# Two edits of a two-block transformer kernel: where the stage areas start, and how the gated linear attention's output products are ordered

## The chip, the cores and the metric

One core of one Trainium2 chip runs the whole program. The metric is the device time of one execution in microseconds (us), lower is better.

## The reference

Two blocks run one after the other on x [1, 512, 1024], all in fp32. The first has two hybrid layers, the second a pooling layer and an attention layer. Cut to what matters here:

```python
def hybrid_layer(x, ...):                       # twice
    h = modulate(rms_norm(x, norm1_g), shift1, scale1)
    rq..rg, gq, gk, gv, glr, gg, fq, fk, fv, ff = split(h @ w_in)
    ret   = silu(rg) * head_group_norm(retention(rq, rk, rv))
    gla_o = silu(gg) * rms_norm(gla(gq, gk, gv, log_a))     # 4 heads, key width 64, value width 128
    fox_o = forgetting_attention(...)
    mixed = sum(sigmoid(h @ w_mg + b_mg) * (branches @ w_br)) @ w_o
    x = x + gate1 * mixed
    u, g = split(h2 @ w_up)
    x = x + gate2 * ((silu(causal_dwconv(u)) * g) @ w_down)

def gla(q, k, v, log_a):                        # chunks of 64 positions
    ...
    _, s_all = lax.scan(step, zeros, (a, kv))   # state after each chunk, 64 x 128 a head
    o = einsum('bnihd,bnhde->bnihe', qc, s_all) # 8 chunks x 4 heads
```

The second block has the same shape of work: norm, mixer, residual, norm, SwiGLU of width 2816, residual.

## The kernel before

Activations lie transposed: 128 features down the partitions and all 512 positions along the row, eight such tiles for 1024 features. The program is written five times over, once for each engine (`TensorSteps`, `ScalarSteps`, `VectorSteps`, and `pool_program`, `sync_program`). One `schedule` walks the first three through the same list of generator steps, so the order of every queue is fixed by the order of the calls.

**Dense products.** Each fp32 product is split in three: a weight tile has a high part `hi` and a low part `lo`, an activation tile as well (`HH`, `HL` for the normed input; others below), and `dot` (L410 to L412) issues hi·high, hi·low and lo·high, each with a 128x128 stationary tile and a moving tile of 512 or 256 columns of type fp32r. SyncE loads weights into a ring of six slots (`raw`), ScalarE copies them to `hi` (L1152), GpSimd subtracts to `lo` (L2463).

**Where tiles lie.** `places` puts the long-lived tiles one after another with `fixed`, each rounded up to 32 bytes, and then a region of 49 x 2048 bytes from `big` on, in which `area(name, tile, ...)` gives every stage its own tiles at `big + tile * 2048`. In the built program `HH` begins at byte 32,896 of each partition, `HL` at 49,280 and `hi` at 90,240, all multiples of 128. `big` is 128,864, which is 1006 x 128 + 96. In the areas are, among others, the moving operands `FH`/`FL` (input of w_down), `ErH`/`ErL`, `EgH`/`EgL`, `EfH`/`EfL` (the three branches), `MH`/`ML` (input of w_o), `PH`/`PL`, `ZH`/`ZL` (pooling) and `YH`/`YL` (attention output).

**Gated linear attention, last part** (`gla_attention`). `weave` gives one step of the gate projections (`gated(l, 0)`, 8 steps) after each step of this generator; the 8 are used up by the time the output products begin, so these have no dense work between them. The four heads lie in pairs: head h uses pair `p2 = h // 2` and row half `hh = h % 2` (partitions 0 to 63 or 64 to 127) of the states `SA` and queries `gq`. A head's output takes 8 matmuls (one for each chunk, 64 rows, 128 stationary columns, 64 moving columns, plain fp32) into PSUM bank `s0` or `s1` (L812). The profile records each plain fp32 matmul twice. Then ScalarE squares the bank into one of two buffers of `glaS` (L1452) and VectorE copies it to `GO` (L2091), TensorE sums the squares by 4 matmuls against `ones` (`colsq`, L486), ScalarE takes the root into `RS` (L1192), VectorE inverts it (L2095), and TensorE spreads it over the partitions (`spread`, L495). The square of head h waits for the sum of head h - 2, whose buffer it takes, and head h's products wait until `GO` of head h - 2 is copied, whose bank they take. When the stage is over, `gated(l, 1)` goes on with dense products.

Of the kernel before, what the change touches and what calls it, by code (L numbers as in the profile page):

```python
# [9 lines left out]
ACT = mybir.ActivationFunctionType  # L10
# [220 lines left out]
class Steps:  # L231
# [8 lines left out]
    def next_chunk(self, pair=False):  # L240
        n = self.n
        if pair and n % NSLOT == NSLOT - 1:
            n += 1
        self.n = n + 1
        return n


def ret_jobs(l):
# [131 lines left out]
class TensorSteps(Steps):  # L380
# [390 lines left out]
    def gla_attention(self, l):  # L771
        e, q, m, t, bank, free = self.e, self.q, self.m, self.t, self.bank, self.free
        LA = t["LA"]
        yield from self.gla_gates(l)
        for u in range(2):
            q.wait_ge(m.vattn.at("la", l, u), free[f"t{u}"])
            for r in range(2):
                mm = e.matmul(bank[f"t{u}"][:, r * 256:r * 256 + 256], t["tail"][:, :], LA[:, u, r * 256:r * 256 + 256],
                              start=True, stop=True)
            mm.then_inc(*m.attn.up(("gd", l, u)))  # L780
            free[f"t{u}"] = m.aattn.at("gd", l, u)
        q.wait_ge(free["s0"])
        for f2 in range(2):
            for r in range(4):
                mm = e.matmul(bank["s0"][:, f2 * 8 + 2 * r:f2 * 8 + 2 * r + 2],
                              LA[:, r // 2, (r % 2) * 256 + f2 * 128:(r % 2) * 256 + f2 * 128 + 128],
                              t["chunk"][:, :], start=True, stop=True)
        mm.then_inc(*m.attn.up(("ga", l)))
        free["s0"] = m.aattn.at("ga", l)
        yield None  # L790
        yield None
        kvb = ("s0", "s1", "t0", "t1")
        for p2 in range(2):
            q.wait_ge(m.vattn.at("gk", l, 0), m.vattn.at("gk", l, 1),
                      *[m.atake.at("gv", l, c, u) for c in range(2) for u in range(2)], *[free[b] for b in kvb])
            for n in range(8):
                c0, r = 64 * (n % 2), n // 2
                mm = e.matmul(bank[kvb[n % 2 + n // 4 * 2]][:, (n // 2 % 2) * 256:(n // 2 % 2) * 256 + 256],
                              t["ED"][c0:c0 + 64, r // 2, (r % 2) * 256 + p2 * 128:(r % 2) * 256 + p2 * 128 + 128],
                              t["gv"][c0:c0 + 64, r, p2 * 256:p2 * 256 + 256], start=True, stop=True)  # L800
            mm.then_inc(*m.attn.up(("gkv", l, p2)))
            for b in kvb:
                free[b] = m.vattn.at("gs", l, p2, 7, 1)
            yield None
        yield None
        for h in range(4):
            p2, hh = h // 2, h % 2
            b = f"s{hh}"
            r = slice(64 * hh, 64 * hh + 64)
            q.wait_ge(m.vattn.at("gs", l, p2, 7, 1), m.atake.at("gq", l, p2), free[b])  # L810
            for n in range(8):
                mm = e.matmul(bank[b][:, n * 64:n * 64 + 64], t["SA"][r, p2, n, :], t["gq"][r, p2, n * 64:n * 64 + 64],  # L812
                              start=True, stop=True)
            mm.then_inc(*m.attn.up(("go", l, h)))
            free[b] = m.vattn.at("go", l, h)
            yield None
            if h >= 1:
                self.gla_sum(l, h - 1)
        self.gla_sum(l, 3)
        free["t1"] = m.aattn.at("gsd", l)  # L820
        yield None
        for h in range(4):
            b = f"t{h % 2}"
            self.spread(t["RS"][:, 4 * h:4 * h + 4], b, m.vattn.at("gr", l), ("gspread", l, h))
            free[b] = m.vattn.at("GO", l, h)
            yield None
# [308 lines left out]
class ScalarSteps(Steps):  # L1135
# [289 lines left out]
    def gla_attention(self, l):  # L1425
        e, q, m, t, bank = self.e, self.q, self.m, self.t, self.bank
        TA, ED, AD, SQ = t["TA"], t["ED"], t["AD"], t["glaS"]
        yield None
        for u in range(2):
            q.wait_ge(m.attn.at("gz", l, u))  # L1430
            e.activation(TA[:, u, :], bank[f"s{u}"][:, :], ACT.Abs).then_inc(*m.aattn.up(("gabs", l, u)))
        for u in range(2):
            q.wait_ge(m.aattn.at("gabs", l, u))
            e.activation(TA[:, u, :], TA[:, u, :], ACT.Exp, scale=-1.0).then_inc(*m.aattn.up(("gexp", l, u)))
        for u in range(2):
            q.wait_ge(m.aattn.at("gexp", l, u))
            e.activation(TA[:, u, :], TA[:, u, :], ACT.Ln, bias=t["one"][:, 0:1]).then_inc(*m.aattn.up(("gln", l, u)))
        yield None
        yield None
        for u in range(2):  # L1440
            q.wait_ge(m.attn.at("gd", l, u))
            e.activation(ED[:, u, :], bank[f"t{u}"][:, :], ACT.Exp, scale=1.0 / 16).then_inc(*m.aattn.up(("gd", l, u)))
        q.wait_ge(m.attn.at("ga", l))
        e.activation(AD[:, 0:16], bank["s0"][:, 0:16], ACT.Exp, scale=1.0 / 16).then_inc(*m.aattn.up(("ga", l)))
        yield None
        yield None
        yield None
        yield None
        yield None
        for h in range(4):  # L1450
            q.wait_ge(m.attn.at("go", l, h), m.stat.at("gsum", l, h - 2) if h >= 2 else None)
            e.activation(SQ[:, h % 2, :], bank[f"s{h % 2}"][:, :], ACT.Square).then_inc(*m.aattn.up(("gsq", l, h)))  # L1452
            yield None
        self.rstd(bank["t1"], 16, 128, m.stat.at("gsum", l, 3), t["RS"][:, 0:16], m.aattn.up(("gsd", l)))
        yield None
        for h in range(4):
            yield None
# [267 lines left out]
class VectorSteps(Steps):  # L1725
# [329 lines left out]
    def gla_attention(self, l):  # L2055
        e, q, m, t, bank = self.e, self.q, self.m, self.t, self.bank
        LA, TA, ED, AD, SA, GO = t["LA"], t["TA"], t["ED"], t["AD"], t["SA"], t["GO"]
# [14 lines left out]
        for p2 in range(2):  # L2072
            q.wait_ge(m.attn.at("gkv", l, p2), m.aattn.at("ga", l))
            for n in range(8):
                for hh in range(2):
                    r = slice(64 * hh, 64 * hh + 64)
# [11 lines left out]
        yield None  # L2088
        for h in range(4):
            q.wait_ge(m.aattn.at("gsq", l, h))  # L2090
            e.tensor_copy(GO[:, h, :], bank[f"s{h % 2}"][:, :]).then_inc(*m.vattn.up(("go", l, h)))  # L2091
            yield None
        RS = t["RS"][:, 0:16]
        q.wait_ge(m.aattn.at("gsd", l))
# [428 lines left out]
def places(nc):  # L2523
    with ExitStack() as ctx:
# [3 lines left out]
        at = [base]  # L2528
        t = {}

        def fixed(name, shape, dt=F32):
            n = int(np.prod(shape[1:])) * 4
            t[name] = nc.alloc_sbuf_tensor_at(name, shape, dt, offset=at[0])
            at[0] += (n + 31) // 32 * 32
# [23 lines left out]
        fixed("NA", [128, 4, 8])  # L2558
        fixed("aG", [128, 24])
        fixed("AA", [128, S])  # L2560
        big = at[0]
        assert big + 49 * TB <= nc.sbuf_usable_end, big + 49 * TB - nc.sbuf_usable_end

        def area(name, tile, shape, dt=F32):
# [74 lines left out]
        bank = {b: ctx.enter_context(nc.psum_tensor(b, [128, S], F32))  # L2639
                for b in ("b0", "b1", "b2", "s0", "s1", "t0", "t1", "o")}  # L2640
        return ctx.pop_all(), t, raw, bank

def build(nc, I, T, out):
    stack, t, raw, bank = places(nc)
    with stack as ctx:
        marks = Marks(lambda name: ctx.enter_context(nc.semaphore(name)))
        K = Kernel(I, T, out, marks, raw, t, bank)
        for program in (tensor_program, scalar_program, vector_program, pool_program, sync_program):
            program(Rehearsal(), K)
        for mark in marks.all():  # L2650
            mark.begin()
        block = ctx.enter_context(nc.Block())

        @block.sync
        def _(e):
            sync_program(e, K)

        @block.tensor
        def _(e):
            tensor_program(e, K)  # L2660

        @block.vector
        def _(e):
            vector_program(e, K)

        @block.scalar
        def _(e):
            scalar_program(e, K)

        @block.gpsimd  # L2670
        def _(e):
            pool_program(e, K)
# [37 lines left out]
```

## Time and profile before

| what | value |
|---|---|
| device time, 3 runs | 3119.80, 3119.99, 3122.06 us (median 3119.99) |
| the profiled execution | 3121.84 us, its span 3120.1 us |
| mean granted TensorE clock | 0.983 |
| TensorE matmul busy / weight load busy | 97% / 81% |
| VectorE, ScalarE, GpSimd busy | 34%, 35%, 38% |
| HBM traffic | 100 GB/s over the span |

The profiled time is 1.7 us longer than the span, which lies around the first and the last instruction. Matmuls overlap, so the duration of one says little; what counts is the distance from one start to the next. L numbers are lines of the kernel before; in the changed one the same code stands 3 to 7 lines further down.

### The profile page before, as it was taken

Reading aid. Unit: us, or ns where it says so; the run is one execution under the profiler, and the core shown is the slowest. Engines: PE = TensorE matmul, PEld = TensorE weight load, DVE = VectorE, ACT = ScalarE, POOL = GpSimd, SP = SyncE. Lnnn points to the kernel's source line nnn. Section 1 sums busy time; section 2 is a strip of 40 time slices with the busy share of each in tenths; the row PEclk is TensorE's granted clock in tenths of the full one; section 3 lists DMA queues with packets and bytes.
Section 4 is the critical chain, followed back from the end, with each engine's and each line's share of the span. In section 5 each row is a group of like instructions: output and inputs, shape, how many; then the busy total and the mean of one; then the engine's idle time right before and its main releaser. Section 6 shows DMA issues by size and latency. Waiting matters only on the chain.

```text
span 3120.1 us, 36402 instructions
## 1 busy us (share of the span) xinstructions
PE 3026.0 (97%) x15435; PEld 2523.2 (81%) x15435; DVE 1056.4 (34%) x1867; ACT 1079.0 (35%) x1643; POOL 1181.2 (38%) x502
## 2 busy tenths in 40 slices
PE   7999999999999999999999999979999999999999
PEld 4887788898888888778888888868888877788887
DVE  2633451255554532231143220463110255531102
ACT  3424333243332433432234332323222266432321
POOL 1422144434445432224434444434444333344442
PEclk9999899999999999989999999989999999999999
DMA  6331253335555422223333333323333322233332
GB/s 208 108 92 51 82 170 100 88 106 184 189 186 169 111 69 61 55 61 95 95 88 101 95 96 95 93 68 95 95 97 91 97 69 67 61 95 95 100 89 75
DMA packets 523798, 315.30 MB, mean 101 GB/s; under 512 B 15954, under 2 KB 496884, under 8 KB 523380
## 3 DMA queue, kind: packets, MB, share of 16 engines
q1 hardware_dynamic: 523636, 312.98, 34.0%
q8 instruction: 122, 2.00, 0.3%
q14 instruction: 40, 0.33, 0.0%
HBM read 310.84 MB, written 2.10 MB: 100 GB/s over the span
## 4 chain that ended last, share of the span: by engine, by line
PE 92%; DVE 4%; ACT 2%; DMA 1%; issue 0%; SPq 0%; ACTq 0%; DVEq 0%
PE b L410 21%; PE b L412 20%; PE b L411 20%; PE o L410 5%; PE o L411 5%; PE o L412 5%; DMA raw<-in_w_in_dram 1%; PE b L451 1%; PE b L452 1%; PE b L453 1%; PE b L555 1%; PE o L727 1%; ACT aT L1283 1%; PE t L495 1%; PE s L812 1%; PE s L621 1%
## 5 line engine op out<-in xcount | busy, mean ns | idle before, releaser
L2463 POOL TENSOR_TENSOR lo<-raw,hi 128x1024 fp32r<-128x1024 f32 (+1 forms) x492 | 1179.1, 2404 | 1900.4 <-ACT hi L1152 1900.1
L410 PE MATMUL b<-HH,hi 128*128 128x512 f32 x1776 | 707.5, 398 | 15.1 <-ACT aT L1283 10.5
L412 PE MATMUL b<-HH,lo 128*128 128x512 f32 x1776 | 694.7, 391 | 0.0
L411 PE MATMUL b<-HL,hi 128*128 128x512 f32 x1776 | 694.3, 391 | 0.0
L1152 ACT ACTIVATE hi<-raw 128x1024 fp32r<-128x1024 f32 (+1 forms) x492 | 508.8, 1039 | 453.9 <-DMA raw<-in_w_down_dram 107.9
L410 PEld LDWEIGHTS b<-HH,hi 128*128 128x128 f32 x1776 | 335.1, 189 | 92.1 <-issue 19.6
L412 PEld LDWEIGHTS b<-HH,lo 128*128 128x128 f32 x1776 | 334.8, 189 | 71.1
L411 PEld LDWEIGHTS b<-HL,hi 128*128 128x128 f32 x1776 | 335.4, 189 | 69.1 <-issue 1.0
L410 PE MATMUL b<-FH,hi 128*128 128x512 f32 (+1 forms) x572 | 212.1, 371 | 0.0
L411 PE MATMUL b<-FL,hi 128*128 128x512 f32 (+1 forms) x572 | 211.4, 370 | 0.0
L412 PE MATMUL b<-FH,lo 128*128 128x512 f32 (+1 forms) x572 | 211.3, 369 | 0.0
L2191 DVE TENSOR_TENSOR CB<-CB,b 128x512 f32<-128x512 f32 x82 | 56.4, 688 | 455.1 <-PE b L412 441.7
L410 PE MATMUL o<-HH,hi 128*128 128x512 f32 x496 | 193.4, 390 | 0.0
L411 PE MATMUL o<-HL,hi 128*128 128x512 f32 x496 | 193.2, 390 | 0.0
L412 PE MATMUL o<-HH,lo 128*128 128x512 f32 x496 | 193.2, 390 | 0.0
L1538 ACT ACTIVATE FH<-CB 128x512 fp32r<-128x512 f32 x88 | 55.6, 632 | 253.7 <-DVE CB L2191 253.7
L410 PE MATMUL b<-hi,HH 128*128 128x256 f32 x480 | 142.8, 297 | 0.4 <-ACT aT L1283 0.4
L411 PE MATMUL b<-lo,HH 128*128 128x256 f32 x480 | 137.4, 286 | 0.0
L412 PE MATMUL b<-hi,HL 128*128 128x256 f32 x480 | 137.2, 286 | 0.0
L1869 DVE SCALAR_TENSOR_TENSOR AA<-raw,CA,AA 128x512 f32<-128x512 f32 x140 | 127.8, 913 | 4.1
L410 PEld LDWEIGHTS b<-FH,hi 128*128 128x128 f32 x572 | 107.7, 188 | 20.0
L412 PEld LDWEIGHTS b<-FH,lo 128*128 128x128 f32 x572 | 107.7, 188 | 19.9
(414 smaller groups left out, 4649.8 us busy)
## 6 DMA issues: line engine op xcount, KB each, us to landing
raw<-in_w_ada_dram SPq DMA_DIRECT2D x96, 512.0 KB, 4.9
raw<-in_w_up_dram SPq DMA_DIRECT2D x88, 512.0 KB, 3.9
raw<-in_w_in_dram SPq DMA_DIRECT2D x80, 512.0 KB, 4.2
raw<-in_w_mg_dram SPq DMA_DIRECT2D x48, 512.0 KB, 3.7
raw<-in_ffn_w_gate_dram SPq DMA_DIRECT2D x44, 512.0 KB, 3.8
raw<-in_ffn_w_up_dram SPq DMA_DIRECT2D x44, 512.0 KB, 3.8
raw<-in_w_down_dram SPq DMA_DIRECT2D x32, 512.0 KB, 3.9
raw<-in_ffn_w_down_dram SPq DMA_DIRECT2D x32, 512.0 KB, 3.9
```

The lines of the kernel that those rows point to most:

```text
L410: e.matmul(out, wh, xh, start=start and k == 0, stop=False)
L411: e.matmul(out, wh, xl, start=False, stop=False)
L412: mm = e.matmul(out, wl, xh, start=False, stop=stop and k == last)
L451: e.matmul(out[:, c], hi[:, k, :], t["HH"][:, k, c], start=(k == 0), stop=False)
L452: e.matmul(out[:, c], hi[:, k, :], t["HL"][:, k, c], start=False, stop=False)
L453: mm = e.matmul(out[:, c], lo[:, k, :], t["HH"][:, k, c], start=False, stop=(k == 7))
L495: mm = e.transpose(self.bank[b][:, r * 128:r * 128 + 128], bc(cols[:, r:r + 1], 128), self.t["ident"][:, :])
L1152: e.activation(t["hi"][:, c % NSLOT, 0:w], K.raw[:, c % NSLOT, 0:w], ACT.Copy).then_inc(*m.hi.up(c))
L1538: e.activation(t["FH"][:, f, :], CB[:, b, :], ACT.Copy).then_inc(*m.atake.up(("fh", i, f)))
L1869: a = e.scalar_tensor_tensor(out=AA[:, :], in0=raw[:, k * 512:k * 512 + 512], scalar=CA[:, kk:kk + 1], in1=AA[:, :], op0=ALU.mult, op1=ALU ...
L2191: e.tensor_tensor(CB[:, b, :], CB[:, b, :], self.out_of(key)[:, :], ALU.mult).then_inc(*m.vtake.up(key))
L2463: e.tensor_tensor(t["lo"][:, s, 0:w], K.raw[:, s, 0:w], t["hi"][:, s, 0:w].bitcast(F32), ALU.subtract).then_inc(*m.lo.up(n))
```

## The change

Two edits. The first rounds `big` up to the next multiple of 128, so every area tile begins 32 bytes later (`FH` at 128,896 = 1007 x 128). The second lets the output products of a head pair alternate: chunk n of the lower row half, then chunk n of the upper. The first pair writes `s0` and `s1`, the second `t0` and `o`, so it no longer waits for the copies of the first pair. All sums of squares come after all products. ScalarE and VectorE keep their order and only read other banks.

```diff
+GLA_BANKS = ("s0", "s1", "t0", "o")
...
-        for h in range(4):
-            p2, hh = h // 2, h % 2
-            b = f"s{hh}"
-            r = slice(64 * hh, 64 * hh + 64)
-            q.wait_ge(m.vattn.at("gs", l, p2, 7, 1), m.atake.at("gq", l, p2), free[b])
+        for p2 in range(2):
+            both = GLA_BANKS[2 * p2:2 * p2 + 2]
+            q.wait_ge(m.vattn.at("gs", l, p2, 7, 1), m.atake.at("gq", l, p2), free[both[0]], free[both[1]])
             for n in range(8):
-                mm = e.matmul(bank[b][:, n * 64:n * 64 + 64], t["SA"][r, p2, n, :], t["gq"][r, p2, n * 64:n * 64 + 64],
-                              start=True, stop=True)
-            mm.then_inc(*m.attn.up(("go", l, h)))
-            free[b] = m.vattn.at("go", l, h)
-            yield None
-            if h >= 1:
-                self.gla_sum(l, h - 1)
+                for hh, b in enumerate(both):
+                    r = slice(64 * hh, 64 * hh + 64)
+                    mm = e.matmul(bank[b][:, n * 64:n * 64 + 64], t["SA"][r, p2, n, :],
+                                  t["gq"][r, p2, n * 64:n * 64 + 64], start=True, stop=True)
+            mm.then_inc(*m.attn.up(("go", l, 2 * p2), ("go", l, 2 * p2 + 1)))
+            for hh, b in enumerate(both):
+                free[b] = m.vattn.at("go", l, 2 * p2 + hh)
+            yield None
+        self.gla_sum(l, 0)
+        self.gla_sum(l, 1)
+        yield None
+        self.gla_sum(l, 2)
+        yield None
         self.gla_sum(l, 3)
...
-            e.activation(SQ[:, h % 2, :], bank[f"s{h % 2}"][:, :], ACT.Square).then_inc(*m.aattn.up(("gsq", l, h)))
+            e.activation(SQ[:, h % 2, :], bank[GLA_BANKS[h]][:, :], ACT.Square).then_inc(*m.aattn.up(("gsq", l, h)))
...
-            e.tensor_copy(GO[:, h, :], bank[f"s{h % 2}"][:, :]).then_inc(*m.vattn.up(("go", l, h)))
+            e.tensor_copy(GO[:, h, :], bank[GLA_BANKS[h]][:, :]).then_inc(*m.vattn.up(("go", l, h)))
...
-        big = at[0]
+        big = (at[0] + 127) // 128 * 128
```

TensorE's queue in the kernel before, at the output products of the first layer (the digit in a bank's name tells it from the others, the digits behind `gq`, `SA`, `ones` and `glaS` only number the tiles):

```order
1474 L812 MATMUL s0<-gq_111,SA_112 128x64 x8
1475 L812 MATMUL s1<-gq_111,SA_112 128x64 x8
1476 L486 MATMUL t1<-ones_58,glaS_121 128x1 x4
1477 L812 MATMUL s0<-gq_111,SA_112 128x64 x8
1478 L486 MATMUL t1<-ones_58,glaS_121 128x1 x4
1479 L812 MATMUL s1<-gq_111,SA_112 128x64 x8
1480 L486 MATMUL t1<-ones_58,glaS_121 128x1 x8
```

The same place in the changed kernel:

```order
1474 L815 MATMUL s0<-gq_111,SA_112 128x64
1475 L815 MATMUL s1<-gq_111,SA_112 128x64
...
1489 L815 MATMUL s1<-gq_111,SA_112 128x64
1490 L815 MATMUL t0<-gq_111,SA_112 128x64
1491 L815 MATMUL o<-gq_111,SA_112 128x64
...
1505 L815 MATMUL o<-gq_111,SA_112 128x64
1506 L489 MATMUL t1<-ones_58,glaS_121 128x1 x16
1507 L498 MATMUL t0<-CON_56,RS_61 128x128 x4
```

The 32 products are the same ones, in another order and with two other banks, and the 16 sums that stood between and behind them now all stand behind them.

## Rows read from the trace of the kernel before

**Rows 1.** The page's section 4: the chain that ended last, by engine.

```profile
PE 92%; DVE 4%; ACT 2%; DMA 1%; issue 0%; SPq 0%; ACTq 0%; DVEq 0%
```

**Rows 2.** Timeline of PE, area tiles, 512 columns: start us, us, instruction; 59 rows between.

```profile
2999.83 0.40 PE L410 MATMUL b<-FH,hi 128*128 128x512 f32 x1
...
3013.83 0.39 PE L410 MATMUL b<-FH,hi 128*128 128x512 f32 x1
```

**Rows 3.** Timeline of PE, HH and HL, 512 columns; 59 rows between.

```profile
2899.84 0.39 PE L412 MATMUL o<-HH,lo 128*128 128x512 f32 x1
...
2913.44 0.39 PE L412 MATMUL b<-HH,lo 128*128 128x512 f32 x1
```

**Rows 4.** Timeline of PE, area tiles, 256 columns; 49 rows between.

```profile
640.92 0.28 PE L410 MATMUL b<-MH,hi 128*128 128x256 f32 x1
...
646.83 0.28 PE L412 MATMUL b<-MH,lo 128*128 128x256 f32 x1
```

**Rows 5.** Timeline of PE, HH and HL, 256 columns; 49 rows between.

```profile
1640.15 0.28 PE L451 MATMUL b<-HH,hi 128*128 128x256 f32 x1
...
1646.15 0.28 PE L453 MATMUL b<-HH,lo 128*128 128x256 f32 x1
```

**Rows 6.** Groups of PE by line and form: xcount | busy us, mean ns | idle before us <-releasers.

```profile
L410 PE MATMUL b<-FH,hi 128*128 128x512 f32 x440 | 174.5, 396 | 0.0
...
L410 PE MATMUL o<-FH,hi 128*128 128x512 f32 x176 | 69.8, 397 | 0.0
```

**Rows 7.** Groups of DVE by line and form, an area tile and `X`, which begins at a multiple of 128.

```profile
L2135 DVE TENSOR_TENSOR SG<-b,SG 128x512 f32<-128x512 f32 x32 | 22.1, 691 | 186.1 <-PE b L412 186.1
...
L1771 DVE TENSOR_TENSOR X<-b,X 128x512 f32<-128x512 f32 x18 | 12.5, 692 | 167.5 <-PE b L412 152.0 <-PE b L907 15.4
```

**Rows 8.** The chain in order of time, a full-height fp32 product of 256 columns.

```profile
337.84 1.73 PE t L778 x8
```

**Rows 9.** Timeline of PE, layer 1: half-height products whose row halves alternate.

```profile
1322.70 1.13 PE L798 MATMUL s<-gv,ED 64*128 64x256 f32 x8
1323.67 1.03 PE L798 MATMUL t<-gv,ED 64*128 64x256 f32 x8
1324.63 0.50 PE L410 MATMUL b<-HH,hi 128*128 128x512 f32 x1
```

**Rows 10.** Timeline of PE, layer 1's output products and sums.

```profile
1339.93 3.39 PE L812 MATMUL s<-gq,SA 64*128 64x64 f32 x32
1343.25 1.05 PE L486 MATMUL t<-ones,glaS 128*128 128x1 f32 x8
1344.23 2.96 PE L812 MATMUL s<-gq,SA 64*128 64x64 f32 x16
...
1352.52 3.57 PE L486 MATMUL t<-ones,glaS 128*128 128x1 f32 x16
```

**Rows 11.** Timeline of ACT, layer 1, squares and root; [idle before <-releaser].

```profile
1345.69 0.58 ACT L1452 ACTIVATE glaS<-s 128x512 f32<-128x512 f32 x1
...
1356.13 0.27 ACT L1192 ACTIVATE RS<-t,eps 128x16 f32<-128x16 f32 x1 [1.60 <-PE t L486]
```

**Rows 12.** Timeline of PE, layer 0, and the spreads that follow.

```profile
364.24 3.39 PE L812 MATMUL s<-gq,SA 64*128 64x64 f32 x32 [0.15 <-DVE SA L2083]
...
383.71 3.93 PE L495 MATMUL t<-CON,RS 128*128 128x128 f32 x16 [0.65 <-DVE RS L2095]
```

**Rows 13.** Timeline of ACT, layer 0.

```profile
371.60 0.58 ACT L1452 ACTIVATE glaS<-s 128x512 f32<-128x512 f32 x1
...
383.09 0.27 ACT L1192 ACTIVATE RS<-t,eps 128x16 f32<-128x16 f32 x1 [1.60 <-PE t L486]
```

**Rows 14.** Stretches: us, PE PEld DVE ACT POOL busy (x), PEclk, DMA share, GB/s.

```profile
1344.50:1345.50 1.00, 1.00 (x9) 1.00 (x9) 0.62 (x1) 0.35 (x1) 0.07 (x1) 0.77 0.00 0
...
1345.50:1360.00 14.50, 13.85 (x62) 12.99 (x63) 4.57 (x8) 5.75 (x8) 2.35 (x1) 0.50 0.00 1
368.00:370.00 2.00, 0.61 (x6) 0.52 (x5) 1.97 (x2) 0.00 (x0) 1.16 (x1) 0.71 0.00 0
```

## The prediction

> **What bounds the kernel now.** I read the chain of work that ended last first: 92% of it is TensorE and waiting for nothing, so the span is the sum of what TensorE issues plus a few stalls [rows 1]. What counts is therefore the distance between starts of the most frequent instructions, and what TensorE waits for where it has no dense work. Both edits concern one of these.
>
> For the distances I took stretches of the timeline in which TensorE runs without a gap. With a moving operand from an area (`FH`, `FL`), 60 steps take 3013.83 - 2999.83 = 14.00 us, or 233.3 ns for each product of 512 columns [rows 2]. With `HH` or `HL` as the moving operand, in the same code with the same kind of weights, 60 steps take 2913.44 - 2899.84 = 13.60 us, or 226.7 ns [rows 3]. With 256 columns it is the other way round: area tiles take 5.91 us for 50 steps, 118.2 ns [rows 4], and `HH` and `HL` 6.00 us, 120.0 ns [rows 5]. Among the wide ones, what sets the two apart in the kernel's own terms is where the tile lies: `HH` and `HL` begin at a multiple of 128 bytes, all area tiles 96 bytes past one. They also lie lower in memory; the trace can't separate the two.
>
> For the stall I read the output products of the gated linear attention. In layer 1 TensorE issues 32 records for heads 0 and 1, 8 for the first sum, 16 for head 2, and so on; the last two sums end 3.57 us after 1352.52 [rows 10], and the root on ScalarE starts at 1356.13 [rows 11]. No dense product stands in between. The granted clock was 0.77 in the stretch 1344.50 to 1345.50, and 0.50 from there to 1360.00: it fell from the 2.4 GHz level to 1.2 GHz at about 1345.0, after some 5 us of these small products [rows 14]. Layer 0 is alike, with the fall between 368 and 370, at about 368.8 by its mean of 0.71 [rows 14].
>
> **The start of the areas.** Nothing is added or removed; each area tile moves by 32 bytes. Wide products with an area operand: `FH` alone stands in 440 + 176 groups of three [rows 6], 1,848 products; counted in the program, the three branches add 576, `MH`/`ML` 240, `ZH`/`ZL` 120, `YH`/`YL` 120, `PH`/`PL` 48: 2,952. If each takes the distance of `HH`, it saves 233.3 - 226.7 = 6.6 ns, together 19.5 us. The bounds are nothing (if the cause lies elsewhere) and 6.6 ns; I take 6.6, since code, weights, type and width are the same and only the tile differs. Narrow products with an area operand number 1,104 (the same tiles in the last output tiles, done in halves). By the nearest rows they go from 118.2 to 120.0 ns, a loss of 1.8 ns each or 2.0 us; the other bound is no change. I take the loss. All these products lie on the chain. For VectorE the start seems not to matter: 691 ns for a sum in an area, 692 for one in `X`, which is at a multiple of 128 [rows 7]; and both are hidden behind TensorE in most of the span. Net for this edit: 19.5 - 2.0 = 17.5 us.
>
> A rule speaks against it. The Trainium skill, "SBUF — State Buffer", section "Door 1: The DMA port swizzle", says that SBUF is read in lines of 16 bytes and that a penalty falls due on crossing to a new line. Byte 128,864 is as good a multiple of 16 as 128,896, so by that rule a contiguous row costs the same before and after, and this edit would bring 0. The sum by the rows goes by the 6.6 ns that they show.
>
> **The alternating products.** The plain fp32 products of full height and 256 columns take 1.73 us for 8 records, 0.216 us each [rows 8]. Those of half height whose halves alternate take 1324.63 - 1322.70 = 1.93 us for 16 records, 0.121 each [rows 9], 1.8 times as fast. So two halves do run beside each other. The output products now take 1343.25 - 1339.93 = 3.32 us for 32 records, 0.104 each [rows 10], with one half after the other. Bounds for the alternating ones are 0.104 (no overlap) and 0.104 x 0.121 / 0.216 = 0.058. I take 0.058, because rows 9 have the same height and the same stationary width: 32 records in 1.9 us.
>
> The Trainium skill, "TensorEngine Tiling (Array Packing)", section "Key Properties", says that tiles of the array are independent, each loading weights and multiplying in parallel. Rows 9 agree, at 1.8 times rather than 2.
>
> Layer 1, step by step. Products of all four heads from 1339.93 take 2 x 1.9 = 3.8 us, to 1343.7; the banks of the second pair are free, so nothing is waited for. The sum of head 0 takes 1344.23 - 1343.25 = 0.98 us [rows 10], to 1344.7. The sum of head 1 waits for its square, which starts at 1345.69 and takes 0.58, to 1346.27 [rows 11]. That square waits in ScalarE's queue for work on the gate tile, not for TensorE, and neither ScalarE's nor VectorE's order changes, so it stays where it is. Then three sums at half clock, 3.57 / 2 = 1.79 us for 8 records [rows 10], end at 1346.27 + 5.37 = 1351.64. The squares of heads 2 and 3 lie beside them: head 3's may start when head 1's sum is done and is needed 1.79 us later. The root then starts at 1351.7 instead of 1356.13: 4.4 us saved. What is late next is again the chain of sums, each behind the other on TensorE.
>
> Layer 0. The products start at 364.24 [rows 12] and would be done with the first sum near 369; the square of head 1 ends at 371.60 + 0.58 = 372.18, three sums end at 377.55, the root starts at 377.6 instead of 383.09 [rows 13]: 5.5 us saved. The spreads and all behind them move up unchanged. Cover: the second pair's products cost nothing as long as they end before head 1's square does, with 1.6 us to spare in layer 1 and 3 in layer 0. Without that cover (no overlap of halves), in layer 1 5.1 of 6.64 us run before the clock falls and the other 1.5 take 3.1, so the products end near 1348.1 and four sums of 1.79 at 1355.3, which saves 0.8; in layer 0, by the same steps, 3.0.
>
> Sum: 17.5 + 4.4 + 5.5 = 27.4 us. The profiled execution took 3121.84, so it becomes 3094.4. Its time is 1.85 above the median of the three runs; against that, 3119.99 - 27.4 = 3092.6, which I round to 3093.
>
> **Rivals.**
> (A) The start doesn't matter, and `HH` is faster for another reason, such as its place in memory. For it: the trace has no tile that differs in its start alone, and the narrow products rank the other way. Against: all area tiles have one distance whatever their offset in the region. Only the products' order counts: 3119.99 - 9.9 = 3110.1. The rule on 16-byte lines leads here too.
> (B) The halves don't overlap at 64 columns, because loading 128 stationary columns is what takes the 0.104 us and only streams overlap. Rows 9 don't refute that fully, as a stream of 256 columns is longer. Saved: 17.5 + 0.8 + 3.0 = 21.3, time 3098.7.
> (C) Slower: a start at a multiple of 128 costs wide products something, as the narrow ones' rows suggest (+1.8 ns), instead of helping. It decides the sign from (9.9 - 2.0) / 2,952 = 2.7 ns for each wide product; at 6.6 the wrong way the time is 3119.99 - 9.9 + 2.0 + 19.5 = 3131.6.
> (D) The clock doesn't fall in the shortened stage. Three sums then take 2.9 us instead of 5.4 and the spreads, 3.93 us at half clock [rows 12], 2.0 less: 4.4 more a layer, 8.8 together, time 3083.8. Against: TensorE waits for head 1's square longer than before, and does no dense work there.
>
> **How the numbers follow.** The forecast has 0.72, with its own range of 3089 to 3098 (1 ns more or less for each wide product, no loss on the narrow ones, a microsecond of the stage). A has 0.12, B 0.07, D 0.06, C 0.02, A and B together 0.01 (3119.99 - 3.8 = 3116.2). A range of 3083 to 3104 takes in the forecast, B and D and a saving on wide products of two thirds, and leaves out 0.15. A measurement of this kernel tells about 0.2%, 6.2 us, from no change. Faster by more: forecast, A, B, D, 0.97. Within: A with B, 0.01. Slower: C, 0.02.
>
> **What the profile would show.** First edit right: 60 steps with `FH` in 13.6 us, and 50 narrow steps in 6.0. If 14.0 stands, A holds. Second: the 32 product records of a pair in about 1.9 us and 64 in one piece; a wait of 1.6 us in layer 1 and 3 in layer 0 for the square of head 1; then 24 sum records in 5.4 us at a granted clock of 0.50; the root 11.8 us behind the first product in layer 1 and 13.4 in layer 0. Products in 3.3 us a pair would be B. Wrong altogether if the square of head 1 moved with the products, or if weights came late to the faster products; SyncE's loads now wait for slots to come free, so I expect none.

## The result, and the profile after

The changed kernel takes 3093.58 us (median of 4 runs, 3091.97 to 3096.79); the kernel before took 3119.89 in the same session. The ratio is 0.991, with a 95% interval of 0.9898 to 0.9923. The forecast was 3093, in a range of 3083 to 3104. The profiled execution took 3096.79 us, its span 3095.0, against 3121.84 and 3120.1.

TensorE still carries the chain, as in [rows 1]:

```profile
PE 92%; DVE 4%; ACT 2%; DMA 1%; issue 1%; SPq 0%; ACTq 0%; DVEq 0%
```

The timeline of PE, area tiles with 512 columns, 60 steps from the first row to the last:

```profile
2358.38 0.39 PE L413 MATMUL b<-FH,hi 128*128 128x512 f32 x1
...
2371.98 0.39 PE L413 MATMUL o<-FH,hi 128*128 128x512 f32 x1
```

That is 13.60 us, 226.7 ns a step, where [rows 2] had 14.00 us; area tiles now go at the pace that `HH` had in [rows 3]. The same view with 256 columns, 50 steps:

```profile
1594.13 0.28 PE L415 MATMUL o<-MH,lo 128*128 128x256 f32 x1
...
1600.13 0.28 PE L414 MATMUL b<-ML,hi 128*128 128x256 f32 x1
```

6.00 us, 120.0 ns, where [rows 4] had 5.91: the small loss came as well. Groups of PE by line and form show the first in sum (busy us, mean ns):

```profile
L413 PE MATMUL b<-FH,hi 128*128 128x512 f32 x440 | 171.5, 390 | 0.0
...
L413 PE MATMUL o<-FH,hi 128*128 128x512 f32 x176 | 68.7, 390 | 0.0
```

They were 174.5 and 69.8 [rows 6]. Overlapping durations add up to more than the time they cover, but here they fell as the distances did: 3.0 us over 440 is 6.8 ns each.

The stage of the output products, timeline of PE, layer 0 and then layer 1 (only the first row of a pair of banks that alternates is shown; the second pair follows in single rows, to 368.08 in layer 0):

```profile
364.56 2.00 PE L815 MATMUL s<-gq,SA 64*128 64x64 f32 x32
...
368.28 1.05 PE L489 MATMUL t<-ones,glaS 128*128 128x1 f32 x8
371.84 5.28 PE L489 MATMUL t<-ones,glaS 128*128 128x1 f32 x24 [2.51 <-ACT glaS L1459]
377.78 3.92 PE L498 MATMUL t<-CON,RS 128*128 128x128 f32 x16 [0.65 <-DVE RS L2102]
...
1329.12 2.00 PE L815 MATMUL s<-gq,SA 64*128 64x64 f32 x32 [0.34 <-DVE SA L2090]
...
1332.83 1.05 PE L489 MATMUL t<-ones,glaS 128*128 128x1 f32 x8
1335.58 4.54 PE L489 MATMUL t<-ones,glaS 128*128 128x1 f32 x24 [1.69 <-ACT glaS L1459]
```

All 64 records of the products take 3.72 us in layer 0 (364.56 to 368.28); before, 32 of them took 3.32 [rows 10]. Then TensorE sums head 0 and waits, 2.51 and 1.69 us, for the square of head 1. ScalarE's timeline of layer 0 shows what that square stands behind:

```profile
366.61 0.60 ACT L1459 ACTIVATE glaS<-s 128x512 f32<-128x512 f32 x1 [0.48 <-PE s L815]
367.10 0.59 ACT L1474 ACTIVATE GT<-b 128x512 f32<-128x512 f32 x1
370.68 0.63 ACT L1476 ACTIVATE ErH<-GT 128x512 fp32r<-128x512 f32 x1 [2.98 <-DVE GT L2119]
371.21 0.58 ACT L1459 ACTIVATE glaS<-s 128x512 f32<-128x512 f32 x1
...
377.17 0.28 ACT L1199 ACTIVATE RS<-t,eps 128x16 f32<-128x16 f32 x1 [1.52 <-PE t L489]
```

Both squares had their input at 366.6; the second waits for two operations on the gate tile, and the latter of these for VectorE, 2.98 us. The root comes 12.61 us behind the first product (377.17 - 364.56). Before, it came 18.85 behind [rows 12, 13]: 6.24 saved. In layer 1 it comes 11.04 behind (1340.15) instead of 16.20 [rows 10, 11]: 5.17 saved. The first dense product moves up by the same amounts, 23.05 to 16.80 and 20.39 to 15.23 us behind the first output product.

Stretches around the fall of the clock (PEclk is the third number from the end):

```profile
368.00:370.00 2.00, 1.33 (x16) 1.18 (x12) 1.97 (x3) 0.00 (x0) 0.77 (x1) 1.00 0.00 1
370.00:381.00 11.00, 8.50 (x38) 7.89 (x39) 5.09 (x10) 5.99 (x8) 2.35 (x1) 0.52 0.17 48
...
1335.00:1337.00 2.00, 1.43 (x11) 1.43 (x11) 1.89 (x3) 1.28 (x4) 0.00 (x0) 0.86 0.00 0
1337.00:1341.00 4.00, 3.35 (x16) 3.26 (x17) 0.95 (x2) 2.46 (x4) 0.00 (x0) 0.50 0.00 0
```

The granted clock still fell from the 2.4 GHz level to 1.2 GHz. By the means it fell at about 370.4 (a mean of 0.52 over 11 us is 0.44 us at full clock and the rest at half) and 1336.4 (0.86 over 2 us: 1.44 at full), 5.9 and 7.3 us behind the first product, where it had been 4.6 and 5.1 [rows 14]. In both layers TensorE was waiting, or had just waited, for the square of head 1.

Over the whole trace, adding up distances from start to start, in us: wide area products 695.0 to 676.6, -18.4, and another -0.7 in two waits of over 3 us among them; narrow area products +1.6; narrow ones with `HH` and `HL` -1.4; those whose moving operand is a weight tile -0.9; wide ones with `HH` and `HL` +3.5 (their usual distance is 227 ns in both; 139 steps against 123 lie between 300 and 500 ns, as at half clock); the two stages -11.4. That is -27.7. The spans differ by 25.1, so everything else took 2.6 us more.

### The profile page after: what moved, and what is told of

Its sections match the earlier page's. It is cut to its first block, busy times and chain, and to the rows that moved or that the text cites. A ratio compares the mean times of both kernels' runs of the same rounds, so it can differ in the third digit from the quotient of the medians.

```text
span 3095.0 us, 36400 instructions
## 1 busy us (share of the span) xinstructions
PE 2999.5 (97%) x15435; PEld 2510.9 (81%) x15435; DVE 1053.0 (34%) x1867; ACT 1079.1 (35%) x1643; POOL 1179.3 (38%) x502
## 4 chain that ended last, share of the span: by engine, by line
PE 92%; DVE 4%; ACT 2%; DMA 1%; issue 1%; SPq 0%; ACTq 0%; DVEq 0%
PE b L413 21%; PE b L415 20%; PE b L414 20%; PE o L413 5%; PE o L415 5%; PE o L414 5%; DMA raw<-in_w_in_dram 1%; PE b L454 1%; PE b L455 1%; PE b L456 1%; PE b L558 1%; PE o L730 1%; DVE SA L2090 1%; ACT aT L1290 1%; PE t L498 1%; DVE W L2232 1%
## 5 line engine op out<-in xcount | busy, mean ns | idle before, releaser
L414 PEld LDWEIGHTS b<-FL,hi 128*128 128x128 f32 x572 | 107.9, 189 | 17.2
```

What stands on the lines that cost most here:

```text
L414: e.matmul(out, wh, xl, start=False, stop=False)
```

## The experiments

All diffs are against the changed kernel unless said otherwise. Times are medians, and each ratio is to the kernel before, run in the same session (3119.9 to 3123.0 us). "Distance" in time is from one product's start to the next, in a mean over a trace's wide products, without gaps of 300 ns or more; for narrow products the text gives the middle value of the trace. In time, two executions of one kernel differ by up to 12.8 us (the kernel before, 3115.04 to 3127.79), so small differences rest on the intervals, not on single runs.

### The two edits apart

**Areas only**, the kernel before with one line changed:

```diff
-        big = at[0]
+        big = (at[0] + 127) // 128 * 128
```

> The kernel before with the areas' start rounded up alone. If the two edits add and the start is worth 6.6 ns on 2,952 wide products less 1.8 ns on 1,104 narrow ones: 17.5 us less than before, about 3102; 60 steps of wide products with FH take 13.6 us and the root of the output stage stays 16.2 and 18.9 us behind the first product. If the start gives nothing by itself: 3120 and 14.0 us.

3103.75 us (4 runs), ratio 0.9942, interval 0.9925 to 0.9958. Wide area products 226.9 ns, narrow ones 120. 0.0058 of 3119.9 is 18 us; the forecast's term was 17.5. The stage is unchanged, yet the root comes 18.74 and 17.23 us behind the first product, where the kernel before had 18.85 and 16.20: in layer 1 the clock fell 3.9 us behind the first product here and 5.1 there. So one trace's stage can differ by a microsecond with nothing changed in it.

**Products only**, the changed kernel without that line:

```diff
-        big = (at[0] + 127) // 128 * 128
+        big = at[0]
```

> The changed kernel with the areas where they were before. If the stage alone gives what the two traces show between first product and root (16.2 to 11.0 us in layer 1, 18.9 to 12.6 in layer 0): 11.4 us less than before, about 3108.5, and 60 steps with FH stay at 14.0 us. If the stage's gain is given back later: 3115 or more.

3114.24 us (9 runs), ratio 0.9975, interval 0.9965 to 0.9985. Wide area products 233.3 ns, as before; root 12.86 and 11.36 us behind, dense products 17.05 and 15.55. The trace saves 6.0 and 4.8 us, the ratio says 8 (5 to 11). The two edits add within the intervals: 0.0058 + 0.0025 = 0.0083, against 0.0090 for both.

### What in the order of the products saves the time

**Head by head**: the second pair's banks and the sums behind all products stay, but the row halves no longer alternate.

```diff
-            for n in range(8):
-                for hh, b in enumerate(both):
+            for hh, b in enumerate(both):
+                for n in range(8):
```

> The changed kernel, but the products of a pair go head by head again (same banks, sums still last). If the overlap of the row halves carries the stage: products take 3.3 us a pair, end after the square of head 1 could start, and the root comes 15.4 us (layer 1) and 15.9 us (layer 0) behind the first product instead of 11.0 and 12.6, 7 to 8 us more than the changed kernel, about 3101. If the new order with four banks carries it and the halves are secondary: the products still hide under the wait for head 1's square, within 2 us of the changed kernel.

3098.88 us (4 runs), ratio 0.9922, interval 0.9908 to 0.9937. Timeline of PE, layer 0:

```profile
365.45 3.05 PE L815 MATMUL s<-gq,SA 64*128 64x64 f32 x29
...
368.45 0.27 PE L815 MATMUL s<-gq,SA 64*128 64x64 f32 x1
368.51 0.27 PE L815 MATMUL t<-gq,SA 64*128 64x64 f32 x1
368.56 0.27 PE L815 MATMUL s<-gq,SA 64*128 64x64 f32 x1
368.62 1.28 PE L815 MATMUL t<-gq,SA 64*128 64x64 f32 x10
...
372.58 6.98 PE L489 MATMUL t<-ones,glaS 128*128 128x1 f32 x32
```

The products now fill 7.13 us (365.45 to 372.58; 6.63 in layer 1) instead of 3.72, and then all 32 sum records run in one piece without a wait. Single records start 0.112 us apart while one half works alone at full clock. At the seams of two heads they do so 0.055 apart, as the rows above show: the next head's first products start beside the last ones of this, though the program doesn't alternate them. The dense products start 18.34 and 17.84 us behind the first product, against 16.80 and 15.23. So the overlap of the halves is worth 1.5 + 2.6 = 4.1 us of the 11.4 (1.3 + 2.3 against the trace of the products alone, whose stage is the changed one too). That lies between the two outcomes that I had expected. The ratios alone don't settle it: 0.9922 and 0.991 differ by 3.7 us, and their intervals overlap. The products themselves are 3.4 and 2.9 us shorter where halves alternate; part of that is lost again because TensorE then waits for the square. The other 7.3 us come with the new banks and the sums moved back together, which ends the waits for squares and copies between the products; no run separates these two.

**Both squares first**: ScalarE squares heads 0 and 1 before it goes on with the gate tile.

```diff
-            yield None
+            if h != 0:
+                yield None
```

> The changed kernel, with ScalarE taking the square of head 1 right behind that of head 0, ahead of the gate tile's work. If head 1's square is what the sums wait for: the wait of 2.5 us in layer 0 and 1.7 us in layer 1 goes, more of the sums run before the clock falls, and the root comes 3 to 5 us sooner in each layer: 3085 to 3088. If the gate work that is now late holds the stage behind it, or the clock falls as early and the square of head 3 then waits: less than 2 us gained in all.

3091.63 us (4 runs), ratio 0.9902, interval 0.9887 to 0.9917. Timeline of ACT, layer 0:

```profile
365.03 1.09 ACT L1459 ACTIVATE glaS<-s 128x512 f32<-128x512 f32 x2
366.00 0.60 ACT L1475 ACTIVATE GT<-b 128x512 f32<-128x512 f32 x1
369.57 0.63 ACT L1477 ACTIVATE ErH<-GT 128x512 fp32r<-128x512 f32 x1 [2.97 <-DVE GT L2120]
370.11 0.58 ACT L1459 ACTIVATE glaS<-t 128x512 f32<-128x512 f32 x1
```

Sum 1 now follows sum 0 directly, and TensorE waits for the square of head 2 instead (1.92 us), which stands where that of head 1 stood. The wait moved by one head. The root comes 1.2 and 1.0 us sooner, not the 3 to 5 that I had expected, and dense products start 15.56 and 14.25 us behind, 1.2 and 1.0 earlier. The runs don't show a gain: the ratios differ by less than their intervals. Only the traces do, and two traces with one and the same stage differ by 0.1 to 1.0 us a layer.

**All four squares first.** As above, with `if h == 3:` in place of `if h != 0:`, so that the gate work comes between the squares and the root.

> The changed kernel, with ScalarE taking all four squares of the output stage ahead of the gate tile's work. If the sums wait only for the squares: sums of heads 2 and 3 no longer wait for the gate work, all four follow the products at 0.9 us each at full clock, and the root comes about 7.5 to 9 us behind the first product in each layer instead of 12.6 and 11.0: 3086 to 3089. If the clock falls before the last sums, or VectorE's copies hold the spreads back: no more than 1 us better than the run with two squares.

3091.64 us (5 runs), ratio 0.991, interval 0.9896 to 0.9923; the same ratio as the change itself. The root comes 9.48 and 9.54 us behind, later than the 7.5 to 9 expected, and dense products 14.48 and 14.54 behind, 2.3 and 0.7 earlier than in the changed kernel. No sum waits long any more. Timelines of ACT, then of DVE, layer 0:

```profile
370.91 0.63 ACT L1477 ACTIVATE ErH<-GT 128x512 fp32r<-128x512 f32 x1 [0.76 <-DVE GT L2120]
371.56 1.28 ACT L1199 ACT_TABLE_LOAD   x1
372.85 0.28 ACT L1199 ACTIVATE RS<-t,eps 128x16 f32<-128x16 f32 x1
```

```profile
372.18 0.68 DVE L2099 COPY GO<-s 128x512 f32<-128x512 f32 x1
372.78 0.68 DVE L2099 COPY GO<-t 128x512 f32<-128x512 f32 x1
373.38 0.68 DVE L2099 COPY GO<-o 128x512 f32<-128x512 f32 x1
373.98 0.24 DVE L2103 RECIPROCAL RS<-RS 128x16 f32<-128x16 f32 x1
```

The sums end near 372.2, but the root waits for the table load, which stands behind the gate work, and the reciprocal for three copies. In the changed kernel the reciprocal followed the root after 0.30 us, here after 1.13.

**The stage before the gate work, on both engines.** ScalarE's `yield None` between the squares and VectorE's between the copies are taken out.

```diff
             e.activation(SQ[:, h % 2, :], bank[GLA_BANKS[h]][:, :], ACT.Square).then_inc(*m.aattn.up(("gsq", l, h)))
-            yield None
...
             e.tensor_copy(GO[:, h, :], bank[GLA_BANKS[h]][:, :]).then_inc(*m.vattn.up(("go", l, h)))
-            yield None
```

> The changed kernel, with all squares and the root on ScalarE, and all copies and the reciprocal on VectorE, ahead of the gate tile's work. In the run with four squares the root came 9.5 us behind the first product and TensorE's next dense product 14.5 us, because the gate work stood ahead of the root, and the copies and the reciprocal behind it. If that is what held it: root 7.5 to 8.2 us, dense product 11.7 to 12.5 us behind the first product (16.8 and 15.2 in the changed kernel), 7 to 8 us less than the changed kernel, near 3086. If the gate work is then late for the next stage, or VectorE's long sums ahead of its first copy hold the banks: less than 3 us.

3093.02 us (4 runs), ratio 0.9909, interval 0.9892 to 0.9926: no better than the change. The root comes 8.93 and 9.88 us behind, the earliest of all in layer 0, and the dense products 15.55 and 16.51. Timeline of PE, then of DVE, layer 0:

```profile
373.80 1.97 PE L498 MATMUL t<-CON,RS 128*128 128x128 f32 x8 [0.65 <-DVE RS L2100]
378.20 1.97 PE L498 MATMUL t<-CON,RS 128*128 128x128 f32 x8 [2.43 <-DVE GO L2105]
```

```profile
375.40 0.69 DVE L2117 TENSOR_TENSOR GT<-GT,RO 128x512 f32<-128x512 f32 x1 [1.66 <-ACT GT L1473]
376.79 0.69 DVE L2119 TENSOR_TENSOR ErL<-GT,ErH 128x512 fp32r<-128x512 f32 x1 [0.69 <-ACT ErH L1475]
377.40 1.40 DVE L2105 SCALAR_TENSOR_TENSOR GO<-GO,PAR,t 128x512 f32<-128x512 f32 x2
```

The gate work didn't vanish. It now stands between the reciprocal and VectorE's products with the spread rows, and the second half of the spreads waits 2.43 us for the bank that these free. My expectation overlooked this: the root came 0.7 and 1.7 us beyond its range, the dense products 3 and 4 us.

### What the start of a tile does

**Areas 64 or 32 bytes past a multiple of 128:**

```diff
-        big = (at[0] + 127) // 128 * 128
+        big = (at[0] + 127) // 128 * 128 + 64
```

> The changed kernel with the areas 64 bytes past a multiple of 128. If rows must begin at a multiple of 128: wide products with FH take 233.3 ns (60 steps in 14.0 us) as in the kernel before, and the time is 17 us above the changed kernel. If a multiple of 64 is enough: 226.7 ns (13.6 us) and no change.

3101.65 us (3 runs), ratio 0.9932, interval 0.9909 to 0.9954. Timeline of PE, 60 steps with area tiles:

```profile
2967.14 0.39 PE L414 MATMUL o<-FL,hi 128*128 128x512 f32 x1
...
2980.88 0.39 PE L414 MATMUL b<-FL,hi 128*128 128x512 f32 x1
```

13.74 us, 229.0 ns: between the two known levels. With `+ 32` instead:

> The changed kernel with the areas 32 bytes past a multiple of 128. If only the distance from a multiple of 128 or of 64 matters: 233.3 ns for a wide product as 96 bytes past gave, 17 us above the changed kernel. By the rule that only lines of 16 bytes count: 226.7 ns.

3108.83 us (5 runs), ratio 0.9957, interval 0.9941 to 0.9972; wide area products 233.4 ns, narrow ones 117. So where the areas start does matter, and 32 past is as bad as 96 past.

**The other tiles moved**, areas left at a multiple of 128. First `HH` and `HL` 96 bytes past one, by moving the small tile `aG` (96 bytes) ahead of them, with 32 bytes behind them:

```diff
         fixed("X", [128, 8, S])
+        fixed("aG", [128, 24])
...
         fixed("HL", [128, 8, S], F32R)
+        at[0] += 32
...
-        fixed("aG", [128, 24])
         fixed("AA", [128, S])
```

> The changed kernel with HH and HL moved 96 bytes further, 96 past a multiple of 128, low in memory as before; all else at a multiple of 128. If the start is the cause: the 6,816 wide products with HH or HL take 233.3 ns instead of 226.7 and the time rises by about 44 us, to 3138; narrow ones with HH fall from 120.0 to 118.2. If the place in memory is the cause: 226.7 ns and 3094.

3141.10 us (3 runs), ratio 1.0055, interval 1.0033 to 1.0078. Timeline of PE, 60 steps with `HH`, then 60 with an area tile:

```profile
2167.15 0.40 PE L414 MATMUL b<-HL,hi 128*128 128x512 f32 x1
...
2181.15 0.40 PE L414 MATMUL o<-HL,hi 128*128 128x512 f32 x1
...
2385.96 0.39 PE L413 MATMUL b<-FH,hi 128*128 128x512 f32 x1
...
2399.91 0.40 PE L413 MATMUL b<-FH,hi 128*128 128x512 f32 x1
```

`HH` at 233.3 ns, as its start would have it. But `FH` takes 13.95 us, 232.5 ns, and begins at a multiple of 128 as in the changed kernel. What differs for it is that the weights moved: `hi` from 90,240 to 90,368. This is where the reading by the start alone fell.

Then the weights 96 past a multiple of 128 (`aG` ahead of `raw`, 32 bytes behind `hi`), everything else at one:

> The changed kernel with raw, lo and hi 96 bytes past a multiple of 128, moving operands all at a multiple. If only the moving operand's start counts: wide products stay at 226.7 ns, and the time within 3 us of the changed kernel. If the loads of the stationary operand pay as well: the distance of wide or of narrow products grows by 1 ns or more, 10 us or more in all.

3158.96 us (2 runs), ratio 1.0115, interval 1.0085 to 1.0144: the largest loss. Timeline of PE, 60 steps with `HH` and `HL`:

```profile
83.25 0.39 PE L414 MATMUL b<-HL,hi 128*128 128x512 f32 x1
...
97.31 0.40 PE L414 MATMUL b<-HL,hi 128*128 128x512 f32 x1
```

14.06 us, 234.3 ns, and 234.2 in the mean of all wide products, with `HH` as with area tiles, though no moving tile had moved.

**All at multiples of 128, weights 128 bytes further** (`aG` and the 32 bytes both ahead of `raw`):

```diff
         fixed("HL", [128, 8, S], F32R)
+        fixed("aG", [128, 24])
+        at[0] += 32
```

> The changed kernel with raw, lo and hi moved up by 128 bytes; every operand of the dense products still begins at a multiple of 128. If a start at a multiple of 128 is what makes a wide product fast: 226.7 ns and no change in time. If it is the distance between the moving tile and the stationary one, taken modulo 256 bytes, that must be zero (it was in the changed kernel; it is 128 here, as for the area tiles of the run with HH shifted, which took 232.4 ns): about 232.4 ns for all 9,768 wide products, some 53 us above the changed kernel, near 3147.

3139.95 us (2 runs), ratio 1.0065, interval 1.0046 to 1.0083. Timeline of PE, 60 steps with `HH`:

```profile
2170.13 0.39 PE L413 MATMUL b<-HH,hi 128*128 128x512 f32 x1
...
2184.13 0.39 PE L413 MATMUL o<-HH,hi 128*128 128x512 f32 x1
```

14.00 us here (the mean over all wide products is 232.8 ns). Every operand begins at a multiple of 128, and only 0.2% of the wide steps take 227 ns or less. The time is 7 us below the expected 3147.

**Three distances in one kernel.** Small tiles are moved so that weights and areas both lie 64 past a multiple of 128 and equal modulo 256, while `HH` lies 64 before the weights and `HL` 96 behind, modulo 256:

```diff
         fixed("HH", [128, 8, S], F32R)
+        fixed("aG", [128, 24])
+        fixed("RS", [128, 16])
         fixed("HL", [128, 8, S], F32R)
+        for name, n in (("foxM", 16), ("foxR", 16), ("ones", 2)):
+            fixed(name, [128, n])
...
-        big = (at[0] + 127) // 128 * 128
+        big = at[0] + 96
```

> The changed kernel with weights and areas both 64 bytes past a multiple of 128 and at distance 0 modulo 256 from each other, HH at distance -64 and HL at +96 from the weights. If the distance to the stationary tile decides: area tiles take 227 ns though they begin at no multiple of 128, HH about 229 (as the areas at +64 did), HL about 234 (as at -96). If the start of each tile by itself decides: area tiles 229, HH 227, HL 233.

3118.90 us (8 runs), ratio 0.9996, interval 0.9985 to 1.0006. Timeline of PE, 60 steps with `HH` and `HL` mixed, then 60 with area tiles:

```profile
1700.25 0.39 PE L413 MATMUL o<-HH,hi 128*128 128x512 f32 x1
...
1714.12 0.39 PE L413 MATMUL b<-HH,hi 128*128 128x512 f32 x1
...
2382.08 0.39 PE L415 MATMUL b<-FH,lo 128*128 128x512 f32 x1
...
2395.68 0.39 PE L415 MATMUL o<-FH,lo 128*128 128x512 f32 x1
```

The area tiles take 226.7 ns a step at 64 past a multiple of 128, the best level, and `HH` with `HL` 231.2 although `HH` itself didn't move. Taken apart, `HH` has 230.6 and `HL` 232.7, each over 1 ns off the expected 229 and 234.

Put together, with the moving tile's start less the stationary tile's, modulo 256:

| moving less stationary | ns a wide product | where |
|---|---|---|
| 0 | 227 | `HH` before; all after; areas of the three distances |
| 64 | 229.1 | areas + 64 |
| -64 | 230.6 | `HH` of the three distances |
| -32 | 233.3, 233.2 | areas before; `HH` moved |
| 32 | 233.4 | areas + 32 |
| 96 | 232.7 | `HL` of the three distances |
| -96 | 234.2 | weights 96 past, `HH` and areas alike |
| 128 | 232.4, 232.8 | areas where `HH` moved; all with weights 128 further |

Neither operand's start alone orders these: moving tiles that lie 128 past a multiple of 256 give 227, 232.4, 232.8 and 234.2, and weights that lie there give 227, 229.1, 233.3 and 233.4. Both starts together do. That it is their difference rests on two rows: 0 was seen with both tiles at 128 past and with both at 192 past, and -32 with 96 against 128 and with 224 against 0. The other rows have one pair of starts each (-96 and 128 on two tiles, but at the same starts). Modulo 256 and not 512: the areas after lie an odd multiple of 256 from the weights, `HH` an even one, and both have 227.

The table orders means, not single steps. At 0, with all tiles at 128 past, 97% of the area steps are 227 ns or shorter. At +64 the three products of a group repeat almost exactly as 232, 226 and 229 ns, though the starts of `FH` and `FL`, and of `hi` and `lo`, are equal modulo 256; with the weights 128 further 28 to 30% of the steps are at most 229 ns and a third 237 to 241. And `HH` and `HL` of the three distances alternate, with single steps from 226 to 235 ns. So something besides this distance acts on a single step, and the values other than that at 0 need not hold in another order of products.

## Why the prediction was right, and where its reason was too narrow

**The areas, 17.5 us.** Right in size: 18 us by the ratio of the areas alone. The wide term was to be 6.6 ns for 2,952 products and the trace has 233.3 to 226.9 ns; the narrow term was to be -2.0 and is -1.6 (in the sign of a saving). The wide area products' summed distances fell by 18.4 us rather than 19.5, since stalls lie among them too.

The reason was only half right. The prediction read "at a multiple of 128 bytes, or 96 past one", and said the trace could not separate that from the place in memory. What the experiments show is that the starts of the moving and of the stationary tile count together, and what they support is their difference modulo 256. Before, `HH`, `HL`, `lo` and `hi` all began 128 past a multiple of 256 and the areas 96 past one. Rounding up by 32 brought the areas to 128 past, that is, to distance 0. Had `at[0]` lain in the other half of 256 bytes, the same line would have brought the areas to distance 128, with 232 to 233 ns, and next to nothing (an estimate from the two rows at 128). That it lay in the right half was luck: nothing in the prediction told the two apart. Rival A, that the start doesn't matter, falls with the areas alone; its suspicion that something besides the moving tile's start was at work was sound. Rival C, a loss at a multiple of 128, is false here, though the kernel with the weights 128 bytes further shows starts at multiples of 128 that cost 20 us against before.

The rule of the Trainium skill, "SBUF — State Buffer", section "Door 1: The DMA port swizzle", on lines of 16 bytes gives all these placements the same cost, since every start is a multiple of 32. The runs differ by up to 65 us (3158.96 against 3093.58), so the measurement decides against using it for this.

**The alternating products, 9.9 us.** Measured 11.4 in the traces, 8 (5 to 11) by the ratio of the products alone. By its steps: 64 records in 3.72 us (3.8 forecast); the square of head 1 done 7.2 and 6.4 us behind the first product (7.9 and 6.3); waits of 2.51 and 1.69 (3 and 1.6); three sums to the root 5.33 and 4.57 (5.37 each). The forecast was short of the trace by 0.7 us a layer, each time for another reason. In layer 0 the gate work on VectorE and ScalarE, and the square behind it, came 0.7 us earlier against the products than in the trace before; the three sums took what was forecast. In layer 1 the clock fell at 1336.4, when the first of the three sums was through, and that sum ran at the 2.4 GHz level; here the term "three sums at half clock" was off, by 0.8 us. That is where the fall happened to lie: in the products-only trace, with the same stage, it came 5.5 us behind the first product instead of 7.3, and the three sums took 5.32 us in either layer.

Rival B, that halves don't overlap, falls: 0.058 us a record where halves alternate and 0.112 where they don't, 1.9 times. Within the run, two records start 6 or 7 ns apart and the next two 0.112 us after them, so there it is twice. The bound of 0.104 that the prediction took from [rows 10] had one seam in it, with its overlap. The Trainium skill, "TensorEngine Tiling (Array Packing)", section "Key Properties", says that tiles operate independently, each loading and multiplying in parallel; the trace agrees. But B was priced wrongly. It left the stage a gain of 0.8 + 3.0 us, and by its roots the head-by-head kernel gains 2.6 and 4.7. In layer 1 I had put its products at 8.2 us (1339.9 to 1348.1), and they took 6.63: three seams overlap, and the clock fell at about 1336.4, 5.5 us behind their start instead of 5.1. Rival D, a clock that stays up, falls by the stretches at 0.50.

What is late next is as forecast the chain of squares and sums. Its two remedies gained 2 to 3 us in the traces and nothing that the runs can tell; the third gave it back at the spreads.

Open: why a distance of 0 is the best, why single steps differ at one distance, and why narrow products rank the other way round (120 ns at 0, 117 to 119 nearly everywhere else). No run separates a conflict between the reads of the two operands from anything else in the loading.

## What to carry to other kernels

Where TensorE alone is the bound, compare the distance of starts for the same instruction on different tiles; 3% between two tiles was worth 18 us here. Before aligning the tile that is slow, write down the starts of both operands modulo 256. In this kernel wide fp32r products were fastest with a difference of 0, and narrow ones up to 3 ns slower there; bring it to 0 where the wide ones outweigh them, measure, and fix it with an explicit offset so that a small tile added elsewhere doesn't undo it. For a short stage on three engines, list what stands in each queue between its steps before moving one of them: wherever the gate work was put, dense products began 14.3 to 16.5 us behind the first output product, against 15.2 and 16.8 with it where it was.

## What was not expected of the hardware

- Shifting only the weight tiles by 96 bytes slows wide products from 227 to 234.2 ns in the mean and the kernel from 3095.0 to 3156.8 us of span. Shifting them by 128 costs three quarters of that, to 3140.6.
- 256-column products don't follow: 120 ns where the wide ones are fastest; where these take over 233, 117 or 118.
- Products on the two row halves overlap at a seam without being written alternately: in the head-by-head kernel some six records of two heads run 0.055 us apart at each of three seams. The records of the two heads alternate there, so by their starts TensorE begins the next head's products before the last ones of the other half have begun. How far ahead it can do so was not tried.
